# Norm sums placed in product loops, first products that share split halves, and four more TensorE taps in the last convolution chunk

## What is computed

```python
y = rms_norm(h, norm1_g[i]) * (1.0 + sc1) + sh1
# layer 0
u = y @ w_pw1 + b_pw1; a, g = split(u); u = a * sigmoid(g)
u = causal_depthwise_conv(u, w_dw, 31 taps) + b_dw
y = silu(layer_norm(u, ln_g, ln_b)) @ w_pw2 + b_pw2
h = h + g1 * y
y = rms_norm(h, norm2_g[i]) * (1.0 + sc2) + sh2
h = h + g2 * ((silu(y @ w_gate) * (y @ w_up)) @ w_down)
# layer 1: S5 scan, gelu, z @ w_glu, za * sigmoid(zg); then the experts; then a final rms_norm
```

## Time and profile before

| what | value |
|---|---|
| time, median of 3 (lowest, highest) | 1613.69 us (1611.99, 1618.89) |
| the profiled execution: time, span | 1611.64 us, 1608.9 us |
| TensorE busy | 1514.5 us (94%), 8591 matmuls |
| VectorE, ScalarE busy | 1286.9 us (80%), 1023.9 us (64%) |
| GpSimd busy | 217.3 us (14%) |
| mean granted clock of TensorE | 0.975 |
| HBM read | 461.15 MB, 287 GB/s over the span |
| chain that ended last | PE 75%, DVE 11%, ACT 4%, POOL 4%, issue 3% |

### The profile page before, as it was taken

The page is one execution under the profiler, slowest core; times in us unless marked ns, Lnnn a source line. Parts: engine busy times, 40 slices in busy tenths (PEclk is TensorE's granted clock), DMA queues, the critical chain, the costliest instruction groups (busy, mean ns, idle before and its releaser), DMA issues.

```text
span 1608.9 us, 23502 instructions
## 1 busy us (share of the span) xinstructions
PE 1514.5 (94%) x8591; PEld 1260.1 (78%) x8591; DVE 1286.9 (80%) x1426; ACT 1023.9 (64%) x1045; POOL 217.3 (14%) x251
## 2 busy tenths in 40 slices
PE   6997999998889699999999999999989999999996
PEld 4776899998659678888888888888877777777774
DVE  4796566556875598898899889889868988899886
ACT  4556555455123487687777687777748777778773
POOL 0771146521770000000000000000000000000000
PEclk9998999999789899999999999999999999999998
DMA  9954386656484689999999999999818999999991
GB/s 307 331 195 168 106 284 231 236 193 236 158 262 148 220 315 367 361 340 370 363 341 357 374 350 355 365 351 354 306 53 314 340 338 344 340 313 338 376 379 40
DMA packets 231208, 463.30 MB, mean 288 GB/s; under 512 B 18255, under 2 KB 57687, under 8 KB 231127
## 3 DMA queue, kind: packets, MB, share of 16 engines
q1 hardware_dynamic: 229591, 461.55, 80.6%
q10 hardware_dynamic: 1536, 0.68, 0.2%
HBM read 461.15 MB, written 1.05 MB: 287 GB/s over the span
## 4 chain that ended last, share of the span: by engine, by line
PE 75%; DVE 11%; ACT 4%; POOL 4%; issue 3%; DMA 1%; SPq 1%; DVEq 0%; ACTq 0%; POOLq 0%
PE bank L2163 12%; PE bank L2166 12%; PE bank L2169 12%; PE bank L1823 12%; DVE wlo L1744 4%; PE bank L1978 3%; PE bank L2305 3%; PE bank L2302 3%; PE bank L2257 2%; PE bank L2258 2%; PE bank L2265 2%; PE bank L2270 2%; PE bank L2269 2%; DVE bank L1315 2%; PE bank L1907 2%
## 5 line engine op out<-in xcount | busy, mean ns | idle before, releaser
L1597 DVE TENSOR_TENSOR wlo<-ring,whi 128x2048 fp32r<-128x2048 f32 x210 | 477.0, 2289 | 68.5 <-PE bank L2169 55.6
L1020 ACT ACTIVATE whi<-ring 128x2048 fp32r<-128x2048 f32 x210 | 400.9, 1918 | 117.7 <-PE bank L2166 117.7
L1744 DVE TENSOR_TENSOR wlo<-ring,whi 128x2048 fp32r<-128x2048 f32 x126 | 283.1, 2281 | 26.2 <-PE bank L2270 25.0
L1117 ACT ACTIVATE whi<-ring 128x2048 fp32r<-128x2048 f32 x126 | 238.4, 1912 | 37.7 <-PE bank L2265 22.9
L2163 PE MATMUL bank<-whi,xe_hi 128*128 128x512 f32 x560 | 219.7, 392 | 7.2 <-ACT whi L1020 7.2
L2166 PE MATMUL bank<-whi,xe_lo 128*128 128x512 f32 x560 | 218.9, 391 | 0.0
L1233 DVE TENSOR_TENSOR ring_lo<-ring,ehi 128x2048 fp32r<-128x2048 f32 x45 | 106.3, 2362 | 58.3 <-ACT ehi L786 58.2
L2169 PE MATMUL bank<-wlo,xe_hi 128*128 128x512 f32 x560 | 150.5, 391 | 0.0
L2163 PEld LDWEIGHTS bank<-whi,xe_hi 128*128 128x128 f32 x560 | 105.8, 189 | 29.4 <-issue 7.3
L2169 PEld LDWEIGHTS bank<-wlo,xe_hi 128*128 128x128 f32 x560 | 105.7, 189 | 22.1
L2166 PEld LDWEIGHTS bank<-whi,xe_lo 128*128 128x128 f32 x560 | 105.8, 189 | 21.9
(11 more groups left out here) (450 smaller groups left out, 2829.4 us busy)
## 6 DMA issues: line engine op xcount, KB each, us to landing
ring<-in_moe_w_gate_dram SPq DMA_DIRECT2D x112, 1024.0 KB, 7.1
ring<-in_moe_w_up_dram SPq DMA_DIRECT2D x112, 1024.0 KB, 6.8
ring<-in_moe_w_down_dram SPq DMA_DIRECT2D x112, 1024.0 KB, 6.7
ring<-in_mod_w_dram SPq DMA_DIRECT2D x24, 2048.0 KB, 9.8
ring<-in_ffn_w_gate_dram SPq DMA_DIRECT2D x11, 1024.0 KB, 6.1
ring<-in_ffn_w_up_dram SPq DMA_DIRECT2D x11, 1024.0 KB, 8.7
ring<-in_ffn_w_down_dram SPq DMA_DIRECT2D x11, 1024.0 KB, 5.2
ring<-in_conv_w_pw_dram SPq DMA_DIRECT2D x8, 1024.0 KB, 12.3
```

Of the source, the lines that this page charges most:

```text
L1020: act.activation(whi[:, n % HI_SLOTS, :], ring[:, s * HW:(s + 1) * HW], ACT.Copy).then_inc(hi_ready, 1)
L1117: act.activation(whi[:, q % HI_SLOTS, :], ring[:, s * HW:(s + 1) * HW], ACT.Copy).then_inc(hi_ready, 1)
L1597: v.tensor_tensor(wlo[:, n % LO_SLOTS, :], ring[:, s * HW:(s + 1) * HW], whi[:, n % HI_SLOTS, :].bitcast(F32), ALU.subtract).then_inc(lo_r ...
L1744: v.tensor_tensor(wlo[:, q % LO_SLOTS, :], ring[:, s * HW:(s + 1) * HW], whi[:, q % HI_SLOTS, :].bitcast(F32), ALU.subtract).then_inc(lo_r ...
```

## The change

- The last chunk of the convolution has 6 TensorE taps and 17 VectorE taps instead of 2 and 21; its four extra diagonals go to a tile of their own.
- The mean's first seven products come before the last S5 transposes; ScalarE's copies 8 to 11 of `mod` move to VectorE, behind `scaled`; both weight splits of VectorE that stood around the centring come later.
- In the pw2 loop and the GLU loop, the square of the chunk before and the norm's sum of two chunks before are taken inside the loop.
- `first_products` makes the first two outputs together, on the first four chunks of the activation, then the rest; between the two, TensorE runs the gate's `mod_sums` (pw2, feed-forward). The early outputs move behind feed-forward product 0.
- VectorE's adds behind the feed-forward start by pairs of chunks (`down_out`), during the last down product.

```diff
@@ scalar (ScalarE)
+                if n == KC - 1:
+                    for k in range(LAST_PE_TAPS):
+                        ins = act.activation(diag_last[:, k, :], ident[:, :], ACT.Copy, scale=dw(DVE_FROM + k, n))
...
+                    if k0 and n:
+                        square(n - 1, hT, sq_late, h4_ready, n)
...
             squares(conv, sq, cent_ready, lambda kc: kc + 1)
             root(1)
-            mod_copy(2 * NORM_MODS)
-            mod_copy(2 * NORM_MODS + 1)
...
+                if n:
+                    square(n - 1, hT, conv, h2_ready, n)
                 if n in (1, 3, 5):
                     split_hi(n // 2 + 2)
-            squares(hT, conv, h2_ready, lambda kc: kc + 1)
+            square(KC - 1, hT, conv, h2_ready, KC)
             split_hi(5)
             root(2)
-            mod_copy(2 * NORM_MODS + 2)
-            mod_copy(2 * NORM_MODS + 3)
@@ vector (VectorE)
+                first = DVE_FROM + (LAST_PE_TAPS if n == KC - 1 else 0)
...
-            split_lo(0)
-            v.wait_ge(mean_sum, 1)
-            link(v.tensor_scalar(nrm[:, 2, :], psum[6][:, 0:T], 1.0 / D, None, ALU.mult))
+            v.wait_ge(sum_ready, 2)
+            link(v.tensor_scalar(nrm[:, 2, :], psum[4][:, 0:T], 1.0 / D, None, ALU.mult))
...
-            split_lo(1)
+            split_lo(0)
             variance(1)
             rsqrt(1)
             scaled(conv, conv)
+            mod_copy(2 * NORM_MODS)
+            mod_copy(2 * NORM_MODS + 1)
             for g in range(2):
                 y_split_lo(y_hi, g)
+            split_lo(1)
...
             scaled(yT, hT)
+            mod_copy(2 * NORM_MODS + 2)
+            mod_copy(2 * NORM_MODS + 3)
...
-            v.wait_ge(down_used, 2 * FBLOCKS)
             for n in range(KC):
+                if n < KC - 2:
+                    v.wait_ge(down_out, n // 2 + 1)
+                else:
+                    v.wait_ge(down_used, 2 * FBLOCKS)
@@ tensor (TensorE)
+            def first_products(outs, high, fresh, one_bank, between=None):
+                for h in range(2):
+                    pe.wait_ge(yhi_ready, fresh + h + 1)
+                    for n, (out, u, k) in enumerate(outs):
+                        _, lo, hi = unit_views(u)
+                        pe.wait_ge(ehi_ready, u + 1)
+                        for kc in range(4 * h, 4 * h + 4):
+                            mm(out, hi[:, kc, k, :], high[:, kc, :], start=kc == 0 and not (one_bank and n), stop=False,
+                               skip_group_check=True)
+                        pe.wait_ge(elo_ready, u + 1)
+                        for kc in range(4 * h, 4 * h + 4):
+                            mm(out, lo[:, kc, k, :], high[:, kc, :], start=False, stop=False, skip_group_check=True)
+                    if h == 0 and between is not None:
+                        between()
+                for out, u, k in outs:
+                    for kc in range(KC):
+                        if kc % 4 == 0:
+                            pe.wait_ge(ylo_ready, fresh + kc // 4 + 1)
+                        ins = mm(out, hi[:, kc, k, :], y_lo[:, kc, :], start=False, stop=kc == KC - 1, skip_group_check=True)
...
+                    if n >= 2:
+                        sum_step(n - 2, 4 * KC, sq_ready, sq_late, sum_ready)
...
             pe.wait_ge(mod_acc, 2 * NORM_MODS)
+            pe.wait_ge(pair_used, KC - 1)
+            for kc in range(KC - 1):
+                sum_step(kc, 0, conv_ready, conv, sum_ready, psum[4])
             s5_transposes(S5_LAST)
-            pe.wait_ge(blk_c, 12)
-            sums(0, conv_ready, conv, mean_sum, psum[6])
+            sum_step(KC - 1, 0, conv_ready, conv, sum_ready, psum[4])
             pe.wait_ge(cent_ready, 1)
             sums(KC, sq_ready, sq, sum_ready)
-            mod_tiles(2 * NORM_MODS, 2 * NORM_MODS + 2)
+            pe.wait_ge(blk_c, 12)
+            mod_partial(2 * NORM_MODS)
+            mod_partial(2 * NORM_MODS + 1)
+            def conv_gate():
+                mod_sums(2 * NORM_MODS)
+                mod_sums(2 * NORM_MODS + 1)
+            for ins in first_products([(psum[4 + n][:, 0:T], u, n) for n in range(2)], y_hi, 0, False, conv_gate):
+                ins.then_inc(pw2_done, 1)
...
+                sum_step(n - 2, 2 * KC, sq_ready, conv, sum_ready)
+            for kc in range(KC - 2, KC):
+                sum_step(kc, 2 * KC, sq_ready, conv, sum_ready)
...
+                    if f == 0:
+                        ins = first_products([(psum[4][:, g * T:(g + 1) * T], u, g) for g in range(2)], y_hi, 2, True, ffn_gate)[1]
...
+                    if f == 0:
+                        early_outputs()
```

More of the change, by code:

```diff
@@ L976, in _ @@
             act.dma_start(bcol[:, :], b_router.rearrange("a e -> e a")).then_inc(wr_in, 16)
[L977 removed]
+            square(KC - 1, hT, sq_late, h4_ready, KC)
             root(4)
@@ L1889, in taps @@
                     pe.wait_ge(conv_ready, n - 1)
+                last = n == KC - 1
                 for k in range(PE_TAPS):
                     ins = mm(psum[n % 2][:, 0:T], diag[:, n % 2, k, :], upad[:, n, k:k + T],
-                             start=k == 0, stop=k == PE_TAPS - 1)
+                             start=k == 0, stop=k == PE_TAPS - 1 and not last)
+                if last:
+                    for k in range(LAST_PE_TAPS):
+                        ins = mm(psum[n % 2][:, 0:T], diag_last[:, k, :], upad[:, n, DVE_FROM + k:DVE_FROM + k + T],
+                                 start=False, stop=k == LAST_PE_TAPS - 1)
                 ins.then_inc(taps_done, 1)
@@ L1945, in _ @@
-            for n in range(KC):
+            pe.wait_ge(blk_c, 12)
[4 more added lines that the diff above has]
+                mod_sums(2 * NORM_MODS + 1)
+            u = UNIT[("pw2", 0, 0)]
+            for ins in first_products([(psum[4 + n][:, 0:T], u, n) for n in range(2)], y_hi, 0, False, conv_gate):
+                ins.then_inc(pw2_done, 1)
+            for n in range(2, KC):
@@ new lines, in _, with ffn_gate, early_outputs @@
+            for kc in range(KC - 2, KC):
+                sum_step(kc, 2 * KC, sq_ready, conv, sum_ready)
+            mod_partial(2 * NORM_MODS + 2)
+            mod_partial(2 * NORM_MODS + 3)
+            def ffn_gate():
+                mod_sums(2 * NORM_MODS + 2)
+                mod_sums(2 * NORM_MODS + 3)
+            def early_outputs():
+                pe.wait_ge(mod_acc, 2 * FFN_MODS)
+                for kc in range(KC):
+                    for c2 in range(2):
+                        for qq in range(4):
+                            rq = slice(32 * qq, 32 * qq + 32)
+                            ins = mm(psum[3][rq, 32 * kc:32 * kc + 32], bblk[c2][:, 4 * kc + qq, :], cT[c2][:, kc, rq],
+                                     start=kc == 0 and c2 == 0, stop=c2 == 1, skip_group_check=True)
+                ins.then_inc(dt_done, 1)
```

86 lines of the change are left out of this document (47 added, 39 removed).

## The result

The changed kernel took 1619.17 us (median of 20 runs, 1613.28 to 1624.67) against 1613.42 us of the kernel before: ratio 1.0031, 95% interval [1.0018, 1.0043]. It is slower by 5 to 6 us, less than the 8.1 us that the prediction set as the bound of a measurable difference. With 20 runs on each side less than that can be told: the interval reaches from 3 to 7 us and is clear of zero. The forecast was 1615.0 us, 1.3 above the median shown before.

What follows compares the result with a forecast made beforehand. TensorE's expert loop passes earlier shifts through; norm waits before it can change. 0.2 + 1.5 - 3.0 + 1.2 - 0.6 - 0.7 = -1.4, slower by 1.4 us; forecast 1615 us on the median's footing, range 1606 to 1621.

Steps and rivals of the forecast that it cites:

- step 2: Convolution's mean and variance: squares 1.8 us earlier, variance's sum 1.6 us dearer at low clock; net gain 0.2 (+1.9 to -1.3).
- step 4: pw2 loop, norm 2, first feed-forward products: 0.3 us gained at full clock, but idling 4.3 us; loss 3.0 (+0.3 to -5.0).
- Step 3: First pw2 products: SiLU starts 2.6 us earlier without ScalarE's copies; gain 4.0 us at full clock, 1.5 taken (+4.0 to -0.5).
- Step 7: GLU end: loop grows 2.65 us, variance waits behind VectorE's eight diagonals and memset; loss 0.7 us.
- What bounds the kernel: TensorE-busy expert loop from 564.2 us passes earlier shifts through at full size; changes lie in four waits for a norm.
- Step 1: Last convolution chunk: four fewer VectorE taps end it 1.59 us sooner; eight extra TensorE passes go into a gap.
- the rival of the gates that feed the low clock: Gates inside first products hold TensorE at 1.2 GHz at pw2, feed-forward and GLU starts: 8.6 us slower, 1622; chance 0.11.
- Step 5: Feed-forward end: adds and squares run during the last down product, so sums start at its end; gain 1.2 us.
- Step 6: GLU start: shared order needs the weights' low half after 4 products; loss 0.6 us, to 2.3 if low clock lasts.
- The clock holds: TensorE keeps full clock from the convolution's mean through the first feed-forward products: 6.1 us faster, 1607.6; chance 0.18.
- Full saving: Three sums leave the path, plus savings on copies, taps and feed-forward end: 15 us, 1599; chance 0.08.

Runs made afterwards that it cites:

- only three parts kept: Changed kernel with only the pw2 start, VectorE's early feed-forward adds and shared first GLU products kept, everything else undone except VectorE's late splits: 0.9972, 1609.49 us.
- the last fillers: Nine more filler products behind norm 3's sums, added to the changed kernel with the mean's order undone and fillers before pw2 and feed-forward: 0.9940, 1603.54 us.

## Why the prediction came out as it did

The time is in the range, and "slower, by less than 8.1 us" is right; that so little could not be told from no change is not, with 20 runs on each side. The size is too small by about 4 us. Of the single steps some held to a few tenths; step 2 lies outside its range and step 4 at the end of its. That the total lies no further off is in part luck: steps 2 and 4 cost 2.6 and 1.9 us more than forecast, and steps 3 and 7 gave back 1.8 and 0.7.

**What bounds the kernel** held. The expert loop passed a shift through; its own length differed, as far as the other profiles tell, by a fall of the clock in one execution.

**Step 1, the taps.** 14 chained taps in 5.57 us against 18 in 7.14 are the 1.6 us. GpSimd's sums were no later than the chain. But the eight added passes were not free: they, too, stand ahead of the transposes. Once the order is undone, 1.1 us of the 1.6 is left in one profile, and 0.1 to 0.2 in two in which the clock is low in the same place as in the kernel compared with.

**Step 2 failed, in its size.** The mechanism was named rightly (ScalarE's copies start later, the weight splits queue behind them, the squares behind those, and TensorE idles 4.2 us; measured 4.25). Three sizes were off. The copies started 3.8 us later against chunk 7 than before, where I had 2.3: the taps ran at the lower clock (2.05 us for four passes, 1.10 in the earlier trace rows), and that pushed the transposes. The working also read one row wrongly: before, the transposes did not release the copies. They were over at 122.08, and the copies stood behind ScalarE's own taps until 124.06, with no idle time ahead of them. So the squares gained 0.44 us and not 1.8. And the variance's sum cost 2.8 more, where I had taken the middle of 0 and 3.2. Together +2.36 us instead of -0.2, outside the range of +1.3 that I gave. What the prediction did not see at all is how much the old order would give back: with it and the taps, this stretch is 14.54 us, 6.3 less than in the changed kernel and 4.0 less than before. In the kernel before, the mean's 16 passes ran at the lower clock (6.73 us), and with the taps kept and the old order they take 3.62. So a part of the 4.0 us comes from where the clock fell in one profile each, and a part perhaps from VectorE's weight split, which the change puts later (its row stands with the kernel whose order was undone). The changed order is worse than the taps are good.

**Step 3 was too careful.** I took 1.5 of a possible 4.0; the profile has 3.28. The mechanism stands as forecast (SiLU directly behind the scaling, idle 2.43 where I had 2.5), and the clock did fall, but only up to the gate. At full clock the third product starts 13.96 to 14.12 us behind the sum's end, with fillers or without, where the working gave 14.4. The working left open what a wait of this length costs, and it is not one number: of eight profiles that waited 2.43 or 2.56 us here, four show the lower clock behind it and take 15.14 to 15.30 us, and four do not and take 13.96 to 14.10.

**Step 4 held, with the clock at its far end.** I had 3.0 us of loss and -5.0 as the bound; the profile has 4.85. At full clock I had a gain of 0.3; with fillers it is 39.38 - 38.70 = 0.7. First half of the activation ready: 12.7 us behind the old loop end forecast, 12.2 measured (29.68 us behind the third product's start, where the old loop ended 17.46 behind it). Product 0 with gate and outputs: 8.95 at full clock by the working, 8.92 and 8.93 with fillers. What failed is the choice within the bound: I let the surcharge end after the first 16 products and a part of the rest, and it ran for 13.7 us. Here the rival of the gates that feed the low clock came true in its size: with the gate inside product 0 the stretch is 13 to 14 us long in each of six profiles without fillers (the changed kernel, and those with taps and order, the order, the sums, the pw2 start and the early adds undone), and with the gate ahead of the wait 3.4 to 6.9 us in three. At pw2 the rival was wrong, for there the clock was back before the gate. With fillers it is wrong on the feed-forward side too: the gate stands in the middle of the products and the clock holds, so narrow passes alone don't bring it down. Whether they prolong a fall, or the wait does that lost its gate and became 3.5 to 4.3 us long, these runs don't tell apart, since each kernel without fillers has both or neither.

The rule in the Trainium skill (TensorE: Matmul & The Clock Gate, section "Loop structure matters more than you think"), that matmuls should follow each other with no long wait, is borne out by these runs for the waits of 4 us: 4.34 us of idle time ahead of the first product cost 5.5 us behind it, and 4.15 us of filler products in their place cost nothing. For those of 2.5 us it held in four profiles of eight. That rule had the sum 1.4 us worse than mine; the steps came out 1.9 us worse.

**Step 5 held**: 1.2 forecast, 1.27 and 1.33 measured. **Step 6 held**: 0.6 and 0.62.

**Step 7 failed by 0.7 us**, harmlessly. The variance does stand behind diagonals and memset, but the diagonals start only 2.11 us later in their stretch than before and not 2.65: of the six sums that I charged at 0.44 us each, the sixth stands behind the last chunk's product on TensorE, in the shadow of its bias and add. Loop and norm together take 39.92 us against 39.89.

**The rivals.** "The clock holds" (6.1 us faster, 0.18) did not happen to the changed kernel, but with the order undone and fillers it did, and more: 7.8 us by the medians, of which the order, which that rival did not have, makes about 3.5 by the ratios (0.9974 and 0.9952). "Full saving" was wrong for the reason given: with the clock held, the sums' place is worth nothing that was measured.

Open stays the 2.4 us by which the medians differ beyond the sum of the steps. It lies in stretches that the change doesn't touch, where the clock falls now here, now there; the profiles show such falls in every kernel, and one profile each can't say how often. That it is chance is not shown.

## What to carry to other kernels

A step that is moved out of a wait leaves the wait behind, and on TensorE the work after a wait of 4 us can run at half the clock for longer than the wait was: price the idle time that an edit makes by what runs behind it, not by its own length. A few products that nobody reads, in just such a wait, turned a loss of 0.3% into a gain of 0.1% here, and in three waits into one of 0.3%; with the order of the mean undone as well it was 0.5%. And before moving sums ahead of transposes, look at what another engine has queued behind these: here two weight splits of 3.70 us in all stood between the transposes and the squares.

## What the runs showed of the hardware that was not expected

- The clock decides the spread as well: over 20 executions of the changed kernel its mean granted clock runs with the time at a correlation of -0.89, over 32 of the kernel before at -0.94. The 5.2 us in the expert loop, whose code is the same, are such a fall.
- The same code can meet a fall in another place. Ahead of chunk 7 the change adds only the four diagonals on ScalarE (1.26 us), and chunk 6 takes 10.12 us with and without them; yet chunk 7 started between 120.04 and 122.58 us in the profiles, and the 16 passes of the mean's sum took 6.73 us in the earlier trace rows and 5.30 us in the kernel with only three parts kept, whose code up to there is nearly that of before.
- How long one stretch takes goes with its time at the lower clock: from norm 3 to the GLU, code that no edit but the last fillers touches, the shortest profile has 80.97 us with 17.1 at the lower clock, the longest 85.45 with 31.8.
- A pass of one column is subject to the clock as a wide one is: the gate's 16 took 1.84 us at full clock and 3.41 at the lower.
